# GELU by one ScalarE function in place of square, cubic, tanh and product steps, in a two-layer trunk

## The chip, the cores and the metric

The program runs on one core of a Trainium2 chip. The metric is the device time of one launch in microseconds; all data is fp32. The engines are named as in the profile: PE is TensorE (PEld its weight loads), DVE VectorE, ACT ScalarE, POOL GpSimd, SP the engine that issues the large DMAs.

## The reference

Two trunk layers run over 128 context and 512 latent tokens of width 1024. Each has a mixing sub-layer, which the change does not touch, and this expert sub-layer, in which every token picks 128 of 16384 single-neuron experts (8 heads of 16):

```python
def peer_ffn(h, p):
    ...
        g = jax.nn.softmax(best, axis=-1).astype(x.dtype)
        act = jax.nn.gelu(jnp.einsum('nhkd,nd->nhk', U[idx], x))
        return jnp.einsum('nhk,nhkd->nd', g * act, V[idx])
```

`jax.nn.gelu` is by default the tanh form, 0.5 a (1 + tanh(0.79788 (a + 0.044715 a^3))).

## The kernel before

The 640 tokens are five tiles of 128. Each layer's expert stage (`stage_experts`) computes them in two ways at once.

**Fetched tiles** (0, 1, 2). GpSimd gathers the rows of `peer_u` and then of `peer_v` for slot k of all 128 tokens, 512 KB a gather, into a ring of buffers (13, later 8). VectorE takes a dot product of each u row (`dot`, L2283) into one column of `acts`. When the 128 columns are there, `cube` makes a(1 + 0.044715 a^2) in three small VectorE steps for each half of 64 columns, ScalarE takes the tanh (L1928), and `weigh` forms (tanh + 1) times (0.5 a share) in two more. Then the v rows are summed with these weights: for tile 0 by TensorE, with diagonal matrices that ScalarE makes (L2006, L2221), for tiles 1 and 2 by VectorE (`add_row`, L2315). A ring buffer is free for the next gather when its row has been used.

**Dense, streamed tiles** (3, 4). All 16384 experts are computed for the 256 tokens, in 128 blocks of 128 experts. SP streams a block's part of both tables, 512 KB each; four u parts and three v parts are buffered. For block b:

- TensorE: `dense_products(b)` (L2202, 16 instructions) into one of two PSUM banks, when `keep_block(b - 2)` has freed it.
- ScalarE, `keep_block(b)`: the tanh of block b - 1 (L1979), then a copy of the products (L1992) and their scaled square (L1993) from PSUM.
- VectorE, `dense_block(b)`: first `gate_acts(b - 1)` (L2348), which multiplies (tanh + 1) into block b - 1 and so releases it to TensorE; then L2356, (square + 1) times a; then L2361, a times the gates (the factor 0.5 is in the gates).
- TensorE: `dense_sums(b)` (L2212, 8 instructions) adds the block's 128 x 1024 product to four PSUM banks.

TensorE's order is fixed: products(b), sums(b - 1), products(b + 1), sums(b). On VectorE and ScalarE the block work stands at fixed places among the rows: `BLOCK_BEHIND` puts block b behind row 40 + 3.66 b of the 512 rows of tiles 1 and 2 (u rows of tile 1 are 0 to 127, its v rows 128 to 255, tile 2 from 256 on). Rows 136 to 219 also carry the ranking of tile 2, one step a row, on VectorE (`rank_step`: maxima, indices and one-hot products, lines 1514 to 1612). Five softmaxes in a layer need ScalarE's Exp (`exp_best`, L1923), two of them amid the dense blocks.

Of the kernel before, what the change touches and what calls it, by code (L numbers as in the profile page):

```python
# [15 lines left out]
ALU = mybir.AluOpType  # L16
# [3 lines left out]
P = 128  # L20
# [1648 lines left out]
def stage_experts(nc, m, l):  # L1669
# [14 lines left out]
    with stage(nc) as sem:  # L1684
# [18 lines left out]
        cube_ready, tanh_ready, gelu_steps, weights_ready = sem("cube_ready"), sem("tanh_ready"), sem("gelu_steps"), sem("weights_ready")  # L1703
# [5 lines left out]
        acts_kept, inner_ready, acts_gated, act_tanh, acts_ready, v_used = (sem(f"dense_{n}") for n in (  # L1709
            "acts_kept", "inner_ready", "acts_gated", "tanh_ready", "acts_ready", "block_added"))  # L1710
# [16 lines left out]
        with nc.Block() as block:  # L1727
            @block.sync
            def _(eng):
# [29 lines left out]
                def load_gates(g):  # L1759
                    if g >= 2:  # L1760
                        eng.wait_ge(acts_gated, GROUP * (g - 1))
# [93 lines left out]
            def _(eng):  # L1855
# [69 lines left out]
                def tanh(i, h):  # L1925
                    cubed = m.cube[:, h * HALF:(h + 1) * HALF]
                    eng.wait_ge(cube_ready, 2 * i + h + 1)
                    eng.activation(cubed, cubed, ACT.Tanh, scale=0.7978845608028654).then_inc(tanh_ready, 1)  # L1928

                def keep_turned(d):  # L1930
# [4 lines left out]
                    eng.activation(m.slot_rows[:, 2, at], m.ps[:, 6 + u % 2, 2 * P:3 * P], ACT.Copy, scale=0.5)  # L1935
                    eng.activation(m.minus_share[:, at], m.ps[:, 6 + u % 2, 2 * P:3 * P], ACT.Copy, scale=-0.5).then_inc(
# [40 lines left out]
                def dense_tanh(b):  # L1977
                    eng.wait_ge(inner_ready, b + 1)
                    eng.activation(m.dense_inner[b % 2], m.dense_inner[b % 2], ACT.Tanh, scale=0.7978845608028654).then_inc(act_tanh, 1)  # L1979

                def keep_block(b):
                    u = block_unit(b)
                    acts = m.ps[:, 6 + u % 2, 0:NT]
                    if b > 0:
                        dense_tanh(b - 1)
                    else:
                        for stored in gates_stored:
                            eng.wait_ge(stored, 16 * CHUNKS // 2)
# [3 lines left out]
                    eng.activation(m.dense_acts[b % 2], acts, ACT.Copy).then_inc(acts_kept, 1)  # L1992
                    eng.activation(m.dense_inner[b % 2], acts.rearrange("p (d t) -> p d t", d=ND), ACT.Square, scale=0.044715 ** 0.5).then_inc(  # L1993
# [3 lines left out]
                tanh(0, 0)  # L1997
                eng.wait_ge(weights_ready, 1)
                for k in range(SLOTS):
                    if k == DIAGS:  # L2000
                        tanh(0, 1)
# [671 lines left out]
```

## Time and profile before

| | |
|---|---|
| time, median of 3 runs | 4896.74 us (4895.52 to 4900.41) |
| the profiled execution | 4902.44 us, of which 4900.6 us is its span |
| PE, PEld busy | 4319.5 us (88%), 2775.0 us (57%) |
| DVE busy | 3534.7 us (72%), 7391 instructions |
| ACT busy | 1158.6 us (24%), 2886 instructions |
| POOL busy | 2105.7 us (43%) |
| DMA | 1280.08 MB, mean 261 GB/s |
| granted TensorE clock, mean | 0.935 |

In a timeline or wait row, the bracket behind an instruction says how long its engine sat idle before it and what ended that idle time. In rows by stretch the DMA share is that of 16 DMA engines; values slightly over 1 are full. The dense blocks take 1480 to 2469 us of the span in the first layer and 3887 to 4875 us in the second.

### The profile page before, as it was taken

How to read it: one execution, taken by the hardware profiler on the slowest of the kernel's cores; microseconds unless marked ns; L12 is line 12 of the kernel's file. 1: busy time of each engine (PE TensorE's matmuls, PEld its weight loads, DVE VectorE, ACT ScalarE, POOL GpSimd, SP SyncE). 2: the span in 40 equal slices, each digit the busy share in tenths (PEclk: the TensorE clock that was granted, in tenths of full speed). 3: DMA queues.
4: the chain of work that ended last, by engine and by line, in shares of the span. 5: the costliest groups of instructions: out<-in, count | busy, mean ns of one | idle time of the engine just before them, and what ended most of it. 6: DMA issues, size and time to landing. Idle time of an engine off the chain costs nothing. (4 is left out here: it accounts for less than half of the span.)

```text
span 4900.6 us, 51932 instructions
## 1 busy us (share of the span) xinstructions
PE 4319.5 (88%) x17506; PEld 2775.0 (57%) x17506; DVE 3534.7 (72%) x7391; ACT 1158.6 (24%) x2886; POOL 2105.7 (43%) x1842
## 2 busy tenths in 40 slices
PE   8989969999848989999979898899996598899998
PEld 3368847544445555655544786565454465555655
DVE  6947665896587898777730676669956788977777
ACT  2112252214551111111110223422254411111111
POOL 0013240764345556665510233326643365566654
PEclk9999969999959999999989998799997799999999
DMA  8700011997689999999931000049976899999998
GB/s 304 240 18 2 1 54 61 337 400 275 241 289 365 408 363 390 407 408 403 405 142 40 6 1 20 35 148 385 368 271 242 303 397 392 365 404 401 407 407 342
DMA packets 390559, 1280.08 MB, mean 261 GB/s; under 512 B 39693, under 2 KB 79749, under 8 KB 387479
## 3 DMA queue, kind: packets, MB, share of 16 engines
q0 software_dynamic: 221184, 805.40, 43.3%
q1 hardware_dynamic: 169112, 471.36, 25.5%
q8 instruction: 142, 2.33, 0.2%
q14 instruction: 121, 0.98, 0.1%
HBM read 1235.01 MB, written 38.99 MB: 260 GB/s over the span
## 5 line engine op out<-in xcount | busy, mean ns | idle before, releaser
L1851 POOL DMA_INDIRECT z<-in_peer_v,experts x768 | 885.3, 1153 | 732.1 <-DVE w L2315 371.8
L1851 POOL DMA_INDIRECT z<-in_peer_u,experts x768 | 883.6, 1151 | 729.4 <-DVE state L2283 451.9
L2202 PE MATMUL ps<-hT,z 128*128 128x256 f32 x4096 | 930.1, 380 | 49.4 <-DMA z<-in_peer_ut 48.9
L2202 PEld LDWEIGHTS ps<-hT,z 128*128 128x128 f32 x4096 | 780.9, 191 | 264.3 <-issue 169.5
L2212 PE MATMUL ps<-w 128*128 128x512 f32 x1360 | 644.7, 618 | 113.2 <-DVE w L2348 112.8
L2315 DVE SCALAR_TENSOR_TENSOR w<-z,state,w 128x1024 f32<-128x1024 f32 x508 | 651.0, 1281 | 76.3 <-DMA z<-in_peer_v,experts 54.7
L2283 DVE CUSTOM_DVE_ANT_0 z<-z,o 128x1024 f32<-128x1024 f32 x512 | 611.6, 1219 | 82.6 <-DMA z<-in_peer_u,experts 81.0
L2212 PEld LDWEIGHTS ps<-w 128*128 128x128 f32 x1360 | 257.2, 196 | 414.6 <-issue 258.2
L2221 PE MATMUL ps<-z,o 128*128 128x512 f32 x1024 | 454.8, 597 | 17.5 <-ACT o L2006 17.5
L1992 ACT ACTIVATE w<-ps 128x256 f32<-128x256 f32 x256 | 98.1, 383 | 1511.5 <-PE ps L2202 1511.5
L2212 PE MATMUL ps<-z,w 128*128 128x512 f32 x688 | 327.7, 621 | 66.0 <-DVE w L2348 64.4
L2221 PEld LDWEIGHTS ps<-z,o 128*128 128x128 f32 x1024 | 190.9, 192 | 232.6 <-issue 232.6
L2283 DVE CUSTOM_DVE_ANT_0 z<-z,ps 128x1024 f32<-128x1024 f32 x256 | 306.0, 1213 | 22.5 <-DMA z<-in_peer_u,experts 19.1
L2356 DVE SCALAR_TENSOR_TENSOR hT<-hT,w 128x256 f32<-128x256 f32 x256 | 109.5, 428 | 278.2 <-ACT hT L1993 278.0
L2187 PE MATMUL ps<-w,z 128*128 128x128 f32 x1024 | 186.9, 346 | 117.7 <-DVE z L2340 70.9
L2187 PEld LDWEIGHTS ps<-w,z 128*128 128x128 f32 x1024 | 173.9, 252 | 161.4 <-issue 147.7
L2212 PEld LDWEIGHTS ps<-z,w 128*128 128x128 f32 x688 | 130.2, 196 | 221.3 <-issue 133.8
L848 POOL TENSOR_TENSOR kn<-kn,neg_half 128x4 f32<-128x4 f32 x20 | 20.1, 1007 | 486.2 <-DVE kn L891 457.6
L464 DVE SCALAR_TENSOR_TENSOR o<-gate,cond,o 128x1024 f32<-128x1024 f32 x160 | 192.4, 1276 | 12.5 <-DMA gate<-in_w_mod 12.5
L401 PE MATMUL ps<-w,hT 128*128 128x512 f32 (+1 forms) x480 | 189.8, 553 | 4.1 <-ACT hT L323 4.1
L583 PE MATMUL ps<-w,hT 128*128 128x512 f32 (+1 forms) x480 | 182.8, 543 | 0.9 <-DVE hT L555 0.9
L858 POOL TENSOR_TENSOR w<-w,const 128x512 f32<-128x512 f32 x60 | 86.5, 1448 | 209.7 <-DVE w L880 117.7
(450 smaller groups left out, 6288.3 us busy)
## 6 DMA issues: line engine op xcount, KB each, us to landing
z<-in_peer_ut SPq DMA_DIRECT2D x256, 512.0 KB, 8.4
w<-in_peer_v SPq DMA_DIRECT2D x170, 512.0 KB, 7.4
z<-in_peer_v SPq DMA_DIRECT2D x86, 512.0 KB, 7.3
gate<-in_w_mod SPq DMA_DIRECT2D x80, 512.0 KB, 4.8
w<-in_w_in SPq DMA_DIRECT2D x10, 2048.0 KB, 10.3
dense_gates<-w SPq DMA_DIRECT2D x8, 2048.0 KB, 9.7
dense_gates<-z SPq DMA_DIRECT2D x8, 2048.0 KB, 10.0
w<-dense_gates SPq DMA_DIRECT2D x16, 1024.0 KB, 18.5
```

Source lines behind the costliest of these rows:

```text
L401: mm = eng.matmul(m.ps[:, 4 + i % 4, 0:cols], m.hT[:, c, t * P:(t + 1) * P], m.w[n % 2][:, c, 0:cols], start=(c == 0), stop=(c == KC - 1))
L464: eng.scalar_tensor_tensor(total, m.mod_piece[i % BUFFERS], m.cond[:, c, s:s + 1], m.mod_bias if c == 0 else total, ALU.mult, ALU.add).the ...
L583: mm = eng.matmul(m.ps[:, 4 + i % 4, 0:cols], m.hT[:, c, k * P:(k + 1) * P], m.w[n % 2][:, c, 0:cols], start=(c == 0), stop=(c == KC - 1))
L1851: eng.indirect_dma_start(slot, None, at_layer_rows(table), bass.IndirectOffsetOnAxis(ap=m.experts[:, i % 2, k:k + 1], axis=0)).then_inc(lo ...
L1992: eng.activation(m.dense_acts[b % 2], acts, ACT.Copy).then_inc(acts_kept, 1)
L2187: mm = eng.matmul(to[:, i * P:(i + 1) * P], m.second_onehot[n % 2][:, i, :], m.first_onehot[n % 2][:, i, :], start=True, stop=True)
L2202: mm = eng.matmul(to[:, 0:NT], m.table_u[b % TABLE_U][:, c, :], m.hT[:, c, D0:TOK], start=(c == 0), stop=(c == KC - 1))
L2212: mm = eng.matmul(m.ps[:, 2 * d + n, :], m.dense_acts[b % 2][:, d * P:(d + 1) * P], m.table_v[b % TABLE_V][:, n * 512:(n + 1) * 512], star ...
L2221: mm = eng.matmul(m.ps[:, 4 + n, :], m.diag[:, k % DIAGS, :], row_j[:, n * 512:(n + 1) * 512], start=(k == 0), stop=(k == SLOTS - 1))
L2283: eng.tensor_tensor_reduce(row_j, row_j, h_first_rows if i == 0 else m.h_row, 1.0, 0.0, ALU.mult, ALU.add, m.acts[:, k:k + 1]).then_inc(us ...
L2315: ins = eng.scalar_tensor_tensor(m.row_sum, row_j, m.weight[:, k:k + 1], m.row_sum, ALU.mult, ALU.add)
L2356: eng.scalar_tensor_tensor(inner, inner, 1.0, acts.rearrange("p (d t) -> p d t", d=ND), ALU.add, ALU.mult).then_inc(inner_ready, 1)
```

## The change

For fetched tiles, `cube` and its three VectorE steps per half go; ScalarE's `gelu(i, h)` reads the dots and writes their GELU to the buffer `cube`, waiting only for the dots; `weigh` is one product with the share. For dense blocks, `keep_block` is one ScalarE instruction that reads PSUM and writes the GELU to `dense_acts`; `dense_block` is the one product with the gates, which now itself releases the block to TensorE; `gate_acts`, `dense_tanh`, the buffer `dense_inner` and four semaphores go. The factor 0.5 leaves the gates' scale.

```diff
-                def tanh(i, h):
-                    cubed = m.cube[:, h * HALF:(h + 1) * HALF]
-                    eng.wait_ge(cube_ready, 2 * i + h + 1)
-                    eng.activation(cubed, cubed, ACT.Tanh, scale=0.7978845608028654).then_inc(tanh_ready, 1)
+                def gelu(i, h):
+                    at = slice(h * HALF, (h + 1) * HALF)
+                    eng.wait_ge(used_v, rows_used(2 * i * SLOTS + (h + 1) * HALF - 1)[0])
+                    eng.activation(m.cube[:, at], m.acts[:, at], ACT.Gelu_apprx_tanh).then_inc(gelu_ready, 1)
...
-                def dense_tanh(b):
-                    eng.wait_ge(inner_ready, b + 1)
-                    eng.activation(m.dense_inner[b % 2], m.dense_inner[b % 2], ACT.Tanh, scale=0.7978845608028654).then_inc(act_tanh, 1)
-
                 def keep_block(b):
...
                     eng.wait_ge(*unit_made("unit", u))
                     if b >= 2:
                         eng.wait_ge(v_used, b - 1)
-                    eng.activation(m.dense_acts[b % 2], acts, ACT.Copy).then_inc(acts_kept, 1)
-                    eng.activation(m.dense_inner[b % 2], acts.rearrange("p (d t) -> p d t", d=ND), ACT.Square, scale=0.044715 ** 0.5).then_inc(
+                    eng.activation(m.dense_acts[b % 2], m.ps[:, 6 + u % 2, 0:NT], ACT.Gelu_apprx_tanh).then_inc(
                         unit_kept.sem, unit_kept.one("unit", u))
...
                 def weigh(i, h):
-                    acts = half(m.acts, h)
-                    eng.wait_ge(cube_ready, 2 * i + h + 1)
-                    o.after(0)
-                    gelu(eng.scalar_tensor_tensor(acts, acts, 0.5, half(m.share, h), ALU.mult, ALU.mult))
                     if i > 0:
                         eng.wait_ge(used_t, SLOTS)
-                    eng.wait_ge(tanh_ready, 2 * i + h + 1)
-                    eng.scalar_tensor_tensor(half(m.weight, h), half(m.cube, h), 1.0, acts, ALU.add, ALU.mult).then_inc(weights_ready, 1)
+                    o.after(0)
+                    eng.wait_ge(gelu_ready, 2 * i + h + 1)
+                    eng.tensor_tensor(half(m.weight, h), half(m.cube, h), half(m.share, h), ALU.mult).then_inc(weights_ready, 1)
...
                 def dense_block(b):
-                    if b > 0:
-                        gate_acts(b - 1)
-                    acts, inner = m.dense_acts[b % 2], m.dense_inner[b % 2]
-                    eng.wait_ge(acts_kept, b + 1)
                     eng.wait_ge(*unit_kept("unit", block_unit(b)))
-                    eng.scalar_tensor_tensor(inner, inner, 1.0, acts.rearrange("p (d t) -> p d t", d=ND), ALU.add, ALU.mult).then_inc(inner_ready, 1)
-                    eng.wait_ge(inner_ready, b + 1)
...
-                    eng.tensor_tensor(acts, acts, gate_part(b), ALU.mult).then_inc(acts_gated, 1)
+                    acts = m.dense_acts[b % 2].rearrange("p (c t) -> p c t", c=CHUNKS)
+                    eng.tensor_tensor(acts, acts, gate_part(b), ALU.mult).then_inc(acts_ready, 1)
```

What stands in a row on the engines, at three places. First VectorE, among the v rows of tile 1 that also carry ranking steps. Before (L2315 is one row, L2348 to L2361 a block's work):

```order
L2348 SCALAR_TENSOR_TENSOR w<-hT,w 128x256
L2356 SCALAR_TENSOR_TENSOR hT<-hT,w 128x2x128
L2361 TENSOR_TENSOR w<-w 128x256
L2315 SCALAR_TENSOR_TENSOR w<-z,state,w 128x1024
L1594 TENSOR_SCALAR ints<-ints 128x2x16
L2315 SCALAR_TENSOR_TENSOR w<-z,state,w 128x1024
```

After (L2327 is the product with the gates, L2294 one row):

```order
L2327 TENSOR_TENSOR w<-w 128x256
L2294 SCALAR_TENSOR_TENSOR w<-z,state,w 128x1024
L1594 TENSOR_SCALAR ints<-ints 128x2x16
L2294 SCALAR_TENSOR_TENSOR w<-z,state,w 128x1024
L1596 TENSOR_SCALAR ints<-ints 128x2x16
```

Of a block's three VectorE instructions one is left. Next ScalarE, around the last Exp of the layer (L1923), amid the dense blocks. Before:

```order
L1992 ACTIVATE w<-ps 128x256
L1993 ACTIVATE hT<-ps 128x2x128
L1923 ACTIVATE o<-o 128x128
L1979 ACTIVATE hT<-hT 128x2x128
L1992 ACTIVATE w<-ps 128x256
```

After (L1984 is the GELU of a block, L1922 the Exp):

```order
L1984 ACTIVATE w<-ps 128x256 x5
L1922 ACT_TABLE_LOAD
L1922 ACTIVATE o<-o 128x128
L1984 ACT_TABLE_LOAD
L1984 ACTIVATE w<-ps 128x256 x29
```

Three instructions a block became one, and the Exp now stands between two table loads that were not there. The whole program has 16 such loads in place of one: each layer has seven (before the first GELU of tile 0, before the Exp of the second softmax, before the GELU of block 0, and on both sides of two Exps amid the blocks), and the second layer begins its Exps with one. Last, the end of the second layer on VectorE. Before:

```order
L2356 SCALAR_TENSOR_TENSOR hT<-hT,w 128x2x128
L2361 TENSOR_TENSOR w<-w,rows 128x256
L2315 SCALAR_TENSOR_TENSOR w<-z,state,w 128x1024 x7
L2348 SCALAR_TENSOR_TENSOR w<-hT,w 128x256
L2320 TENSOR_TENSOR o<-w,gate 128x1024
```

After:

```order
L2294 SCALAR_TENSOR_TENSOR w<-z,state,w 128x1024 x4
L2327 TENSOR_TENSOR w<-w,rows 128x256
L2294 SCALAR_TENSOR_TENSOR w<-z,state,w 128x1024 x7
L2299 TENSOR_TENSOR o<-w,gate 128x1024
L2300 TENSOR_TENSOR x<-x,o 128x1024
```

The release of the last block to TensorE (L2348) stood behind the last seven rows; now it is L2327, ahead of them.

## Rows read from the trace of the kernel before

**Rows 1.** The page's first part: busy us, share of the span, instructions by engine.

```profile
PE 4319.5 (88%) x17506; PEld 2775.0 (57%) x17506; DVE 3534.7 (72%) x7391; ACT 1158.6 (24%) x2886; POOL 2105.7 (43%) x1842
```

**Rows 2.** Dense-block stretches: length, busy by engine, clock, DMA share, GB/s.

```profile
1679.70:1866.50 186.80, 159.90 (x537) 100.71 (x536) 174.40 (x383) 24.61 (x68) 98.19 (x80) 0.98 0.99 373
...
3887.40:4086.60 199.20, 182.48 (x613) 116.06 (x612) 162.61 (x353) 28.84 (x82) 118.96 (x95) 0.98 1.00 387
4086.60:4273.00 186.40, 159.47 (x535) 100.57 (x534) 173.98 (x382) 24.20 (x67) 97.36 (x79) 0.98 0.99 374
4273.00:4874.60 601.60, 563.21 (x1898) 358.94 (x1897) 451.71 (x671) 85.42 (x241) 361.30 (x289) 0.99 1.02 403
...
4300.00:4340.00 40.00, 38.35 (x135) 25.14 (x135) 31.41 (x37) 6.03 (x17) 26.50 (x21) 1.00 1.03 411
```

**Rows 3.** The same, VectorE's line 2361 (one per dense block) alone.

```profile
4086.60:4273.00 186.40, 8.94 (x22) 0.98 0.99 374
4273.00:4874.60 601.60, 34.02 (x80) 0.99 1.02 403
```

**Rows 4.** VectorE's waits (us, times, longest): two stretches, then whole span.

```profile
DVE hT L2356 <- ACT hT L1993: 11.5, 8, 2.2
...
DVE hT L2356 <- ACT hT L1993: 86.5, 65, 4.5
...
DVE o L2320 <- PE ps L2212: 8.5, 2, 4.5
```

**Rows 5.** Timeline of one dense block: start, length, instruction, idle before.

```profile
4177.90 0.41 DVE L2348 SCALAR_TENSOR_TENSOR w<-hT,w 128x256 f32<-128x256 f32 x1
4178.24 0.42 DVE L2356 SCALAR_TENSOR_TENSOR hT<-hT,w 128x256 f32<-128x256 f32 x1
...
4178.37 3.70 PE L2212 MATMUL ps<-z,w 128*128 128x512 f32 x8 [1.35 <-DVE w L2348]
...
4178.69 0.42 DVE L2361 TENSOR_TENSOR w<-w 128x256 f32<-128x256 f32 x1
...
4179.03 1.28 DVE L2315 SCALAR_TENSOR_TENSOR w<-z,state,w 128x1024 f32<-128x1024 f32 x1
...
4181.91 3.62 PE L2202 MATMUL ps<-hT,z 128*128 128x256 f32 x16
...
4185.56 0.38 ACT L1992 ACTIVATE w<-ps 128x256 f32<-128x256 f32 x1 [6.46 <-PE ps L2202]
...
4186.33 0.43 DVE L2356 SCALAR_TENSOR_TENSOR hT<-hT,w 128x256 f32<-128x256 f32 x1 [0.43 <-ACT hT L1993]
```

**Rows 6.** Timeline of the second layer's end.

```profile
4874.58 0.42 DVE L2361 TENSOR_TENSOR w<-w,rows 128x256 f32<-128x256 f32 x1
...
4874.93 9.62 DVE L2315 SCALAR_TENSOR_TENSOR w<-z,state,w 128x1024 f32<-128x1024 f32 x7
...
4884.46 0.42 DVE L2348 SCALAR_TENSOR_TENSOR w<-hT,w 128x256 f32<-128x256 f32 x1
...
4884.93 6.71 PE L2212 MATMUL ps<-w 128*128 128x512 f32 x8 [7.35 <-DVE w L2348]
```

**Rows 7.** Timeline of the start of tile 0's weighted sum, second layer.

```profile
3480.47 0.31 ACT L1923 ACTIVATE o<-o 128x128 f32<-128x128 f32 x1 [4.37 <-DVE o L1550]
...
3482.40 0.26 ACT L1928 ACTIVATE state<-state 128x64 f32<-128x64 f32 x1 [1.62 <-DVE state L2295]
...
3483.42 2.44 ACT L2006 ACTIVATE o<-const,state 128x128 f32<-128x128 f32 x8 [0.76 <-DVE state L2305]
...
3483.92 5.33 PE L2221 MATMUL ps<-z,o 128*128 128x512 f32 x7 [8.46 <-ACT o L2006]
```

**Rows 8.** Timeline of ScalarE at the span's start.

```profile
0.73 1.28 ACT L305 ACT_TABLE_LOAD   x1 [0.73 <-PEq L2667]
```

**Rows 9.** The chain that ended last, 4255 to 4300: start, length, what.

```profile
4256.05 3.70 PE ps L2212 x8
...
4272.66 5.40 PE ps L2212 x8
```

More of the change, by code:

```diff
@@ L1708, in stage_experts @@
         u_loaded, v_loaded = [sem(f"table_u_loaded{k}") for k in range(TABLE_U)], [sem(f"table_v_loaded{k}") for k in range(TABLE_V)]
-        acts_kept, inner_ready, acts_gated, act_tanh, acts_ready, v_used = (sem(f"dense_{n}") for n in (
-            "acts_kept", "inner_ready", "acts_gated", "tanh_ready", "acts_ready", "block_added"))
+        acts_ready, v_used = sem("dense_acts_ready"), sem("dense_block_added")
         def place_of(j):
@@ L1991, in keep_block @@
                         eng.wait_ge(v_used, b - 1)
-                    eng.activation(m.dense_acts[b % 2], acts, ACT.Copy).then_inc(acts_kept, 1)
-                    eng.activation(m.dense_inner[b % 2], acts.rearrange("p (d t) -> p d t", d=ND), ACT.Square, scale=0.044715 ** 0.5).then_inc(
+                    eng.activation(m.dense_acts[b % 2], m.ps[:, 6 + u % 2, 0:NT], ACT.Gelu_apprx_tanh).then_inc(
                         unit_kept.sem, unit_kept.one("unit", u))
                 exp_best(0)
-                tanh(0, 0)
+                gelu(0, 0)
                 eng.wait_ge(weights_ready, 1)
@@ L2000, in _ @@
                     if k == DIAGS:
-                        tanh(0, 1)
+                        gelu(0, 1)
                     if k == HALF:
@@ L2020, in _ @@
                     if k % (2 * SLOTS) == HALF + 2:
-                        tanh(1 + k // (2 * SLOTS), 0)
+                        gelu(1 + k // (2 * SLOTS), 0)
                     if k == SHARES_BEHIND[3]:
@@ L2031, in _ @@
                     if k % (2 * SLOTS) == SLOTS - 1:
-                        tanh(1 + k // (2 * SLOTS), 1)
-                dense_tanh(NKEY - 1)
+                        gelu(1 + k // (2 * SLOTS), 1)
             @block.tensor
@@ L2244, in _ @@
                 h_first_rows = m.ps[:, 0:2, :].rearrange("p b n -> p (b n)")
-                o, gelu, res = Order(eng, route_steps), Order(eng, gelu_steps), Order(eng, sums)
+                o, res = Order(eng, route_steps), Order(eng, sums)
                 def gate_output(i):
@@ L2417, in _ @@
                         dense_block(b)
-                cube(1, 1)
                 for k in range(SLOTS):
@@ L2595, in place @@
     m.dense_acts = [wall[:, 7168 + b * NT:7168 + (b + 1) * NT] for b in range(2)]
-    m.dense_inner = [m.hT[:, ND * b:ND * (b + 1), 0:P] for b in range(2)]
     m.table_u = [zall[:, (8 + b) * D:(9 + b) * D].rearrange("p (c n) -> p c n", c=KC) for b in range(TABLE_U)]
```

33 lines of the change are left out of this document (5 added, 28 removed).

## The prediction

> **What bounds the kernel now.** I read the busy shares first, then the dense-block stretches one by one, then VectorE's waits, then the timeline of one block. Over the whole span TensorE is busy 88%, VectorE 72%, ScalarE only 24% [rows 1], so shortening ScalarE's work alone gains nothing. The changed block code runs in some 990 us of each layer, and there the question is what sets the pace. Away from the ranking steps a 40 us window moves 411 GB/s at a DMA share of 1.03 [rows 2]: the transfers are full, and 411 is my measure of full. Over 601.6 us the last stretch still averages 403 [rows 2], and its blocks come every 601.6 / 79 = 7.6 us (80 records, the first and the last at its edges) [rows 3]. In such a stretch a faster VectorE cannot help. The middle stretch differs: 22 blocks in 186.4 us [rows 3], 8.5 us each, at 374 GB/s in the second layer and 373 in the first, with VectorE busy 174 of 186 us [rows 2]. These are the rows that also carry tile 2's ranking. VectorE is late there, a late row frees its ring buffer late, and the next gather starts late. The remaining 11.5 us of VectorE's time there are one wait, for ScalarE's square of the block's products [rows 4].
>
> The block's timeline shows why VectorE waits on anything. Its first instruction, L2348 at 4177.90, releases the previous block; TensorE, idle for 1.35 us by then, runs the sums (4178.37) and the next products (4181.91), ScalarE gets them at 4185.56, and VectorE's L2356, ready earlier, waits 0.43 us and starts at 4186.33 [rows 5]. So TensorE waits for VectorE once a block, and VectorE for TensorE and ScalarE once a block, in turn.
>
> **The change, part by part.**
>
> *VectorE in a dense block.* L2348 starts at 4177.90, and the row behind the block's three instructions at 4179.03: 1.13 us. L2361 alone takes 4178.69 to 4179.03, 0.34 us [rows 5]. So 0.79 us a block goes, 17.4 us over the middle's 22 blocks.
>
> *The lockstep.* sums(b) is now released by block b's own product, one place of 3.66 rows earlier. TensorE can run the next products while VectorE does rows, and VectorE should find its GELU made. This takes away most of the 11.5 us in the middle, and of the 86.5 us in the last stretch [rows 4]; what is late next there is the rows, by the full DMA.
>
> *Middle stretch.* VectorE's own bound falls to 186.4 - 11.5 - 17.4 = 157.5 us, 7.2 us a block. The transfers' bound is 186.4 x 374 / 411 = 169.6 us, so it decides: at most 16.8 us saved, and in the first layer 186.8 x (1 - 373 / 411) = 17.3 us. The low end is 0, if the gathers' round trip and not VectorE sets the pace. I take 13 a layer, nearer the high end, since VectorE's 94% busy leaves little room for another cause: 26 us.
>
> *First and last stretch.* By the same reckoning 199.2 x (1 - 387 / 411) = 11.6 us and 601.6 x (1 - 403 / 411) = 11.7 us are missing from full [rows 2]. The first has more VectorE work than the last (the ranking of tile 1 among its rows), so I take a third of the one, 4 us, and a sixth of the other, 2 us, and as much in the first layer: 12 us together. Their ends are 0 and 47.
>
> *The end of a layer.* Now L2348 stands behind the last seven rows: it starts at 4884.46, TensorE has been idle 7.35 us and takes 6.71 us for the last eight instructions instead of 3.70 [rows 5, 6], and VectorE waits 8.5 us in all, in two places, 4.5 us at most, for these sums before it can add them [rows 4]. After the change the release stands ahead of the seven rows, which take 9.62 us [rows 6]; the sums fit under them. Both waits go whole: 8.5 us. What is late next is VectorE's own residual steps.
>
> *ScalarE.* A block's three instructions become one of about 0.38 us [rows 5]. On the path only the second PSUM read counts, about 0.3 us, and it lies under the transfers: nothing.
>
> *Fetched tiles.* The five small VectorE steps of a half become one. At the start of tile 0's sum, from the end of the Exp (3480.78) to ScalarE's first diagonal (3483.42) there are 2.6 us [rows 7] with the steps of both halves. Of that TensorE waits for all, so it is worth costing: after the Exp a table load of 1.28 us [rows 8] and a GELU of 0.26 us end at 3482.3, and one product and the diagonal follow, about 0.8 us earlier than now. The other five halves of a layer stand among rows and cost under 1.3 us each (half of those 2.6); they lie under the transfers. Nothing for all; bounds 15 us of gain, 3 of loss.
>
> *Table loads.* The order of ScalarE shows 15 new ones. The one load in the trace takes 1.28 us [rows 8]. All but the one just costed stand where ScalarE idles: between blocks it is idle 6.46 us [rows 5], and during the diagonals eight are made ahead. So 0 to 15 x 1.28 = 19 us of loss; I take 0.
>
> The Trainium skill, "ScalarE: Activation LUTs", section "What ACT_TABLE_LOAD costs", gives 1283 ns for the load and about 1380 ns more for a drain, 2.66 us a switch, and its section "Table sets: the hidden batching unit" says to batch calls by set, which this change does the opposite of. The row agrees on the load; no row here shows the drain. By the page the upper end of the loss is an estimated 40 us, which would leave 6 of the 46 us below, and the first diagonal would come 0.6 us later rather than 0.8 earlier.
>
> *New waits.* `gelu(i, h)` waits on ScalarE for the dots of its half with block GELUs queued behind it, and TensorE behind those. They wait only if TensorE is ahead of VectorE's rows by then, that is for something that is not late: nothing. SP's table loads stay in their order.
>
> **Sum.** 26 + 12 + 8.5 = 46.5 us, from the profiled execution's 4902.4: 4856. That execution is 5.7 us above the median of the runs shown (4896.7), so **4850 us**.
>
> **Rivals.**
>
> *The transfers hide it all.* If the pace of the middle is the gathers' round trip, VectorE's 28.9 us become idle time and only the ends of the layers gain, 8.5 us: 4888. For it: GpSimd's gathers are 8 deep at most. Against it: the same ring gives 411 GB/s elsewhere [rows 2].
>
> *The table loads are exposed.* 19 us of the 46.5 are given back: 4869. Against it: ScalarE's idle gaps.
>
> *The transfers fill up everywhere.* All that is missing from full is recovered, 34 + 47, and 8.5 at the ends: 4896.7 - 89 = 4807. Against it: the last stretch is held up by its own mix of transfers too, which nothing here changes.
>
> *TensorE loses its clock; slower.* TensorE now runs ahead and then stands idle in every block. The clock is granted at 0.98 in all stretches [rows 2], but single sums at the lower level (1.2 in place of 2.4 GHz, in part) take 5.40 us in place of 3.70 [rows 9]. From start to start a block costs TensorE 3.54 + 3.65 = 7.2 us [rows 5]. The pace now is 987.2 us for 127 blocks, 7.8 us. If more than one block in three pays the 1.7 us, TensorE is slower than that; with every second, 8.05 us a block, 254 blocks lose 71 us less the 8.5: about 4959. Against it: in the middle stretch TensorE is already idle 27 of 186 us, at 0.98 [rows 2].
>
> **How the numbers follow.** The forecast's case, 4828 to 4866, has 0.72; the exposed loads (whose time lies in the range) 0.07; the full transfers, where they pass 4828, 0.06; all hidden 0.10; slower 0.05. Under 4828 and over 4882 lie 0.19, so the range is 4828 to 4882. A measurement of this kernel tells 0.2%, about 10 us, from no change. Faster by more: 0.72 + 0.07 + 0.06 = 0.85; within it 0.10; slower 0.05.
>
> **What would show it.** Right: the middle stretch at 170 to 175 us and over 400 GB/s; VectorE's wait for ScalarE there and in the last stretch nearly gone, with waits for fetched rows in its place; no idle time before the last residual steps; 16 table loads, next to none of them waited for. Wrong: a middle stretch of the old length with an idle VectorE (then the gathers' round trip sets it), a granted clock under 0.95 in the stretches, or loads of which VectorE or TensorE waits for more than a few.

## The result, and the profile after

| | before | after |
|---|---|---|
| median of 4 runs | 4896.13 us (4892.95 to 4900.41) | 4830.85 us (4829.40 to 4835.61) |
| ratio, 95% interval | | 0.9868 (0.9851 to 0.9885) |
| profiled execution | 4902.44 us | 4831.36 us |

The change saves 65 us by the medians, 71 us between the two profiled executions. The forecast was 4850 us; the measured time is 19 us below it and inside its range. Mechanism and sign were right, two terms of the sum were too small, and one step was wrong in a way that the time of the changed kernel alone doesn't show.

The page's busy shares of the changed kernel, which answer to [rows 1], and three of its groups (busy us, mean ns of one, idle time ahead of them and what ended it):

```profile
PE 4298.0 (89%) x17506; PEld 2774.6 (57%) x17506; DVE 3339.4 (69%) x6831; ACT 1002.6 (21%) x2389; POOL 2022.9 (42%) x1842
...
L2294 DVE SCALAR_TENSOR_TENSOR w<-z,state,w 128x1024 f32<-128x1024 f32 x508 | 651.2, 1282 | 251.4 <-DMA z<-in_peer_v,experts 245.0
L2273 DVE CUSTOM_DVE_ANT_0 z<-z,o 128x1024 f32<-128x1024 f32 x512 | 623.8, 1222 | 285.3 <-DMA z<-in_peer_u,experts 282.6
...
L1984 ACT ACTIVATE w<-ps 128x256 f32<-128x256 f32 x256 | 98.3, 384 | 1728.2 <-PE ps L2192 1728.2
```

VectorE lost 195 us of work, and over the whole span it now waits some 530 us in its rows for fetched data. The same three stretches of the second layer as in [rows 2], cut where the product with the gates (now L2327) of blocks 0, 26, 48 and 127 begins; columns as in [rows 2]:

```profile
3848.90:4040.10 191.20, 182.25 (x625) 118.53 (x624) 143.04 (x292) 13.27 (x31) 109.41 (x94) 0.99 1.02 403
4040.10:4211.40 171.30, 158.66 (x544) 102.05 (x543) 158.16 (x339) 10.83 (x25) 106.49 (x80) 0.99 1.03 407
4211.40:4808.00 596.60, 561.25 (x1880) 359.39 (x1880) 392.37 (x506) 32.45 (x83) 317.56 (x290) 0.98 1.03 406
```

Before, these moved 387, 374 and 403 GB/s; now all three move 403 to 407, and the first layer's 400, 406 and 406. The granted clock moved by no more than 0.01. VectorE's longest waits in the middle and in the last of these stretches (engine, what it waited for, us in all, times, longest), against [rows 4]:

```profile
DVE w L2294 <- DMA z<-in_peer_v,experts: 13.4, 20, 1.2
...
DVE w L2294 <- DMA z<-in_peer_v,experts: 106.0, 124, 2.2
DVE z L2273 <- DMA z<-in_peer_u,experts: 93.4, 99, 1.5
```

No wait for ScalarE is left in either; 11.5 and 86.5 us of it stood there. VectorE now waits for rows. TensorE still waits for VectorE's product with the gates, 12.2 us in the middle and 30.6 us in the last stretch, where it waited 26.7 and 39.7 us for L2348 before. The chain of work that ended last shows what stands behind VectorE: in the last stretch 81% of it is gathers of rows in flight; before, these were 30% of it, and TensorE's instructions 39%.

**Where the 71 us went.** The stretches between the same products, in us:

| from block to block | before, layers 1 and 2 | after | saved |
|---|---|---|---|
| 0 to 26 (first) | 199.7, 198.7 | 191.8, 191.2 | 7.9, 7.5 |
| 26 to 48 (middle) | 186.8, 186.9 | 168.5, 171.4 | 18.3, 15.5 |
| 48 to 127 (last) | 602.4, 601.6 | 596.8, 596.5 | 5.6, 5.1 |
| last product to the residual steps of layer 1, to the span's end in layer 2 | 16.75, 26.0 | 12.5, 21.3 | 4.25, 4.7 |

That is 59.9 us in the dense stretches and 9.0 at the layers' ends. Block 0 of the first layer comes 4.8 us earlier, of which 3.5 are there ahead of the first instruction that the change touches, so they are no part of it; 2.4 us are lost between layer 1's residual steps and block 0 of layer 2. 59.9 + 9.0 + 4.8 - 2.4 = 71.3. Without the 3.5 the profiled pair gives 67.8, near the 65 of the medians. The rest of the 4.8 is not shown to come from the change either: in a second profile of the kernel before, *before_again* below, block 0 comes at 1473.2 us, ahead of the changed kernel's 1475.3.

### The profile page after: what moved, and what is told of

It is laid out like the page before. It is cut to its first block and busy times, and to the rows that moved or that the text cites. A ratio compares the mean times of both kernels' runs of the same rounds, so it can differ in the third digit from the quotient of the medians.

```text
span 4829.3 us, 50351 instructions
## 1 busy us (share of the span) xinstructions
PE 4298.0 (89%) x17506; PEld 2774.6 (57%) x17506; DVE 3339.4 (69%) x6831; ACT 1002.6 (21%) x2389; POOL 2022.9 (42%) x1842
## 5 line engine op out<-in xcount | busy, mean ns | idle before, releaser
L1850 POOL DMA_INDIRECT z<-in_peer_v,experts x768 | 851.6, 1109 | 733.2 <-DVE w L2294 371.0
L1850 POOL DMA_INDIRECT z<-in_peer_u,experts x768 | 834.2, 1086 | 750.7 <-DVE state L2273 501.2
L2294 DVE SCALAR_TENSOR_TENSOR w<-z,state,w 128x1024 f32<-128x1024 f32 x508 | 651.2, 1282 | 251.4 <-DMA z<-in_peer_v,experts 245.0
L2273 DVE CUSTOM_DVE_ANT_0 z<-z,o 128x1024 f32<-128x1024 f32 x512 | 623.8, 1222 | 285.3 <-DMA z<-in_peer_u,experts 282.6
L1984 ACT ACTIVATE w<-ps 128x256 f32<-128x256 f32 x256 | 98.3, 384 | 1728.2 <-PE ps L2192 1728.2
L858 POOL TENSOR_TENSOR hT<-hT,const 128x512 f32<-128x512 f32 x60 | 85.6, 1433 | 199.4 <-DVE hT L880 103.7
## 6 DMA issues: line engine op xcount, KB each, us to landing
z<-in_peer_ut SPq DMA_DIRECT2D x256, 512.0 KB, 10.6
```

The lines of the kernel that those rows point to most:

```text
L858: eng.tensor_tensor(heads4(m.ct[d][j % 2][:, :]), m.lh[d][:, :].rearrange("p (h k x) -> p h k x", h=4, k=2)[:, :, 0, :], bc(const(m, f"lev ...
L1850: eng.indirect_dma_start(slot, None, at_layer_rows(table), bass.IndirectOffsetOnAxis(ap=m.experts[:, i % 2, k:k + 1], axis=0)).then_inc(lo ...
L1984: eng.activation(m.dense_acts[b % 2], m.ps[:, 6 + u % 2, 0:NT], ACT.Gelu_apprx_tanh).then_inc(unit_kept.sem, unit_kept.one("unit", u))
L2273: eng.tensor_tensor_reduce(row_j, row_j, h_first_rows if i == 0 else m.h_row, 1.0, 0.0, ALU.mult, ALU.add, m.acts[:, k:k + 1]).then_inc(us ...
L2294: ins = eng.scalar_tensor_tensor(m.row_sum, row_j, m.weight[:, k:k + 1], m.row_sum, ALU.mult, ALU.add)
```

## The experiments

**Theory.** In the kernel before, the dense stretches were held under the transfers' ceiling by a lockstep of TensorE, ScalarE and VectorE. The change takes three things out of it: VectorE's 0.79 us a block, the late release, and ScalarE's second read of PSUM. With enough of them gone the transfers set the pace at some 407 GB/s, and more gives nothing. **Rivals:** one of the three alone carries the gain; the table loads cost part of what could be had; the fetched tiles' shorter chain carries a part; the ceiling is not the transfers but something else that the change left alone.

Each kernel was timed beside the kernel before on the same chip, and a ratio is to that. The chips differ: the kernel before takes 5009 and 5011 us where late_release, vector_steps_back, both_back, dense_only, no_switch and loads_moved ran, and 4895 to 4898 us elsewhere. In the changed kernels that were profiled on both kinds of chip, the difference lies outside the dense stretches (block 0 of the first layer comes at 1519 to 1533 in place of 1475 us), so ratios and stretch lengths are compared below, and times across chips are not.

### One cause put back at a time

*late_release* is the changed kernel with the old place of the release: block b - 1 is released by a one-column copy at the start of block b's VectorE work.

```diff
+                def release(b):
+                    eng.wait_ge(acts_gated, b + 1)
+                    eng.tensor_copy(m.hT[:, 0, 0:1], m.dense_acts[b % 2][:, 0:1]).then_inc(acts_ready, 1)
                 def dense_block(b):
+                    if b > 0:
+                        release(b - 1)
...
-                    eng.tensor_tensor(acts, acts, gate_part(b), ALU.mult).then_inc(acts_ready, 1)
+                    eng.tensor_tensor(acts, acts, gate_part(b), ALU.mult).then_inc(acts_gated, 1)
```

> The changed kernel, but the release of a dense block to TensorE is again issued by VectorE one block later, by a copy of one column ahead of the next block's product (under 0.1 us of VectorE a block). VectorE's 0.79 us a block stays saved. Theory V (VectorE's freed time makes the gain): the middle stretch stays near 170 us and only the end of a layer loses its 4.5 us and a little elsewhere, 4840 to 4848 us. Theory R (the earlier release makes it): VectorE waits for the GELU of the block again as before, the first and last stretches fall back to 199 and 602 us and most of the gain goes, 4870 to 4890 us.

Measured: 0.9909 (0.9886 to 0.9933), 44.6 us less than before. Its middle stretch (columns as in [rows 2]):

```profile
4158.90:4331.80 172.90, 157.61 (x535) 100.00 (x533) 159.28 (x360) 10.40 (x25) 105.47 (x80) 0.99 1.02 400
```

And VectorE's only wait in it:

```profile
DVE w L2334 <- ACT w L1985: 15.1, 10, 2.6
```

The wait for ScalarE is back, 15.1 us, and the stretch still takes 172.9 us, 14.0 less than before: VectorE's own time went by 14.7 us, and that is what shows. The last stretches take 597.0 and 596.8 us, as in the changed kernel, though VectorE's wait for ScalarE is back there too (78.3 us in the second layer). The first stretches, 195.8 and 195.3 us, lie halfway between the changed kernel's 191.5 and the 199 of before. The second layer's end is back at 25.0 us after the last product, where the changed kernel has 21.3. So neither theory's time came: 0.9909 of 4896 us is 4851, between the 4840 to 4848 of V and the 4870 to 4890 of R.

*vector_steps_back* leaves the release early and puts two VectorE steps of a block's size back, behind the product and on another buffer, so that VectorE has its old work and nothing waits for it but the rows.

```diff
                     eng.tensor_tensor(acts, acts, gate_part(b), ALU.mult).then_inc(acts_ready, 1)
+                    for k in range(2):
+                        eng.wait_ge(padded, 2 * b + k)
+                        eng.scalar_tensor_tensor(m.hT[:, 2:4, 0:P], m.hT[:, 0:2, 0:P], 1.0, m.hT[:, 0:2, 0:P], ALU.add, ALU.mult).then_inc(padded, 1)
```

> The changed kernel with the early release, but two VectorE steps of 128x256 that nobody needs behind each dense block's product (some 0.8 us a block, as before the change). Theory V: the middle stretch goes back towards 186 us in each layer, 4850 to 4865 us, while first and last stretch keep their gain, since VectorE now waits there for fetched rows. Theory R: no change, 4829 to 4838 us.

Measured: 0.9874 (0.9853 to 0.9895), 58.8 us less. Its middle stretch, in which VectorE's only wait is one of 1.3 us for a fetched row:

```profile
4159.60:4334.30 174.70, 157.25 (x536) 99.69 (x536) 173.80 (x384) 10.41 (x24) 98.59 (x80) 1.00 1.02 398
```

VectorE works 173.8 of 174.7 us: there it is the bound, at what the kernel before leaves without its 11.5 us of waiting, 186.9 - 11.5 = 175.4. So with ScalarE's shorter turn beside it, either of VectorE's two causes gives most of the middle (14.0 and 12.3 us in the second layer, against 15.5 for all of it), and they don't add up, because the transfers stand close behind either. No run has one of them without ScalarE's part.

On the whole time theory R's forecast came: 0.9874 of 4896 us is 4834, and the interval overlaps the changed kernel's, so the time doesn't show that VectorE's saved steps are worth anything beside the early release. Only the stretches do: in sum they take 1923.5 us, where the changed kernel's take 1916.1. The middle ones are longer by 6.6 and 3.2 us and the first by 1.6 and 2.2, but the last ones are shorter, 592.7 and 594.3 in place of 596.8 and 596.5 us, at a granted clock of 0.99 and 1.00 in place of 0.98. No run explains that.

*both_back* has both: the release late, by a step of the old size, and one step ahead of the product. What is left of the change in a block is ScalarE's side: one instruction in place of three, one read of PSUM in place of two.

```diff
+                    eng.scalar_tensor_tensor(acts, acts, 1.0, acts, ALU.mult, ALU.max).then_inc(acts_ready, 1)
...
                 def dense_block(b):
+                    if b > 0:
+                        release(b - 1)
...
+                    eng.scalar_tensor_tensor(m.hT[:, 2:4, 0:P], m.hT[:, 0:2, 0:P], 1.0, m.hT[:, 0:2, 0:P], ALU.add, ALU.mult).then_inc(padded, 1)
+                    eng.wait_ge(padded, b + 1)
```

> The changed kernel with both taken back: one padding step ahead of the product, and the release one block late by a full-size step. What is left of the change is ScalarE's single function and the fetched tiles. If the two parts explain the gain: 4885 to 4896 us, with the stretches at their old lengths. If ScalarE's shorter work counts for itself: 4860 to 4880 us.

Measured: 0.9959 (0.9945 to 0.9973), 20.8 us less than before. The stretches are 196.6 and 195.8, 185.6 and 184.5, 598.7 and 598.6 us: most of the way back to the kernel before, not all. The middle one moves 380 GB/s. In the last stretch VectorE waits for ScalarE again, less than the 86.5 us before (another 10.4 us ahead of the same instruction have no releaser in the profile):

```profile
DVE hT L2334 <- ACT w L1985: 61.3, 50, 3.9
```

So 0.4% is left that neither of VectorE's two causes holds, as the second forecast, 4860 to 4880 us, had it. The prediction had given nothing to what remains.

*scalar_too* is both_back with the second read: a Square of the products behind the GELU, into a buffer that nothing uses, and only this frees the PSUM bank and starts VectorE.

```diff
-                    eng.activation(m.dense_acts[b % 2], m.ps[:, 6 + u % 2, 0:NT], ACT.Gelu_apprx_tanh).then_inc(
+                    eng.activation(m.dense_acts[b % 2], m.ps[:, 6 + u % 2, 0:NT], ACT.Gelu_apprx_tanh)
+                    eng.activation(m.hT[:, 4 + 2 * (b % 2):6 + 2 * (b % 2), 0:P], m.ps[:, 6 + u % 2, 0:NT].rearrange("p (d t) -> p d t", d=ND), ACT.Square).then_inc(
                         unit_kept.sem, unit_kept.one("unit", u))
```

> The kernel of both_back with one thing more taken back: ScalarE reads each dense block's products from PSUM a second time (a square that nobody uses, 0.28 us more until the block is released to VectorE and the bank to TensorE). both_back kept 0.4% of the 1.4% gain, 16 us of it in the dense stretches. If that rest is ScalarE's shorter turn: the time comes back to that of before, ratio 0.998 to 1.000. If the rest is something else (the tanh step, the fetched tiles): ratio 0.995 to 0.997 as in both_back.

Measured: 0.9996 (0.9987 to 1.0005), over 11 and 15 runs: 4894.05 against 4895.32 us. The time of the kernel before is back; the stretches take 1970.7 us in sum, and 1976.1 and 1973.2 in the two profiles of the kernel before. The timeline of scalar_too around the end of one block's products:

```profile
4185.06 0.42 DVE L2327 SCALAR_TENSOR_TENSOR w<-w 128x256 f32<-128x256 f32 x1
...
4185.15 0.38 ACT L1985 ACTIVATE w<-ps 128x256 f32<-128x256 f32 x1 [7.86 <-PE ps L2194]
4185.43 0.38 ACT L1986 ACTIVATE hT<-ps 128x256 f32<-128x256 f32 x1
...
4185.53 3.70 PE L2204 MATMUL ps<-w 128*128 128x512 f32 x8 [0.42 <-DVE w L2327]
4185.84 0.43 DVE L2335 SCALAR_TENSOR_TENSOR hT<-hT 128x256 f32<-128x256 f32 x1 [0.36 <-ACT hT L1986]
```

And VectorE's longest wait in its last stretch, against 86.5 us before:

```profile
DVE hT L2335 <- ACT hT L1986: 77.7, 61, 2.9
```

VectorE starts when the second read ends, 4185.81, and not when the first does: 4185.43 - 4185.15 = 0.28 us later in each block. 0.28 x 256 blocks would be 72 us if all of it counted. By the ratios of both_back and scalar_too it counts for some 0.4%, about 18 us, and their intervals don't overlap. Of these 18, the six stretches show 10.8 (1959.9 and 1970.7 us in sum); where the others lie was not found. What the second read alone would cost in the changed kernel, where the transfers are full, no run shows.

### The fetched tiles

*dense_only* has the change in the dense blocks alone. The fetched tiles keep `cube`, the tanh and the two steps of `weigh`:

```diff
-                    eng.wait_ge(used_v, rows_used(2 * i * SLOTS + (h + 1) * HALF - 1)[0])
-                    eng.activation(m.cube[:, at], m.acts[:, at], ACT.Gelu_apprx_tanh).then_inc(gelu_ready, 1)
+                    eng.wait_ge(cube_ready, 2 * i + h + 1)
+                    eng.activation(cubed, cubed, ACT.Tanh, scale=0.7978845608028654).then_inc(tanh_ready, 1)
```

> The change made for the dense blocks alone; the fetched tiles keep square, cubic, tanh and product steps (tanh without a table load more, if it is in the same table as the new function). If the fetched tiles are worth nothing, as predicted: 4829 to 4836 us, at most 2 us for the two starts of tile 0's sum. If their small steps on VectorE count: 4840 us or more.

Measured: 0.9848 (0.9824 to 0.9872). The full change gave 0.9868 and, run again, 0.9864. The interval takes both in, and its stretches (192.2 and 190.1, 170.7 and 171.4, 594.3 and 598.3 us) are the full change's within 3 us each and 1 us in sum. The fetched tiles' part is worth nothing that can be measured, as forecast; the interval would hide some 12 us.

### The table loads

*no_switch* takes the loads away: the five softmaxes of a layer use Tanh in place of Exp, so that their shares are not the reference's, and from tile 0's first GELU on ScalarE needs no other set of functions in the expert stage. 4 loads are left of 16, two of them ahead of that first GELU.

```diff
-                    eng.activation(m.shifted, m.shifted, ACT.Exp).then_inc(sems.best_exp_ready, 1)
+                    eng.activation(m.shifted, m.shifted, ACT.Tanh).then_inc(sems.best_exp_ready, 1)
```

> The changed kernel with the softmax's exponential in the expert stage replaced by tanh (so its shares are not the reference's): only 4 table loads are left of 16. If the 12 loads are exposed: 12 x 1.28 = 15 us less, 4815 us. If they are hidden but for the one ahead of block 0 of each layer, where ScalarE loads only after it has waited for the products: 2 to 3 us less, 4828 us.

Measured: 0.9865 (0.9843 to 0.9887), the changed kernel's ratio. Twelve loads fewer, nothing gained: 15 us less would have given about 0.984. A gain of 2 to 3 us is too small for this interval.

*loads_moved* keeps them and moves them off the waits: a one-column GELU ahead of block 0's wait, and the two Exps amid the blocks issued behind the next block's GELU.

```diff
                     if b == 0:
+                        eng.activation(m.hT[:, 0, 0:1], const(m, "ident", 0, 1), ACT.Gelu_apprx_tanh)
...
-                    if k == SHARES_BEHIND[3]:
-                        exp_best(3)
```

> The changed kernel with a GELU of one column ahead of the wait for block 0's products, so that its table load runs during that wait, and with the two Exps amid the dense blocks issued behind the next block's GELU instead of ahead of it, so that the GELU no longer stands behind ScalarE's wait for the ranking (9.0 and 9.8 us in the second layer). If the transfers set the pace everywhere: 2 to 3 us less (the load ahead of block 0), 4828 us. If the block held behind the Exp costs a stall of its own: 3 to 8 us less, 4823 to 4828 us.

Measured: 0.9858 (0.9836 to 0.9881). Between the two kernels lie 2 us of 4942; both say that the loads cost nothing measurable. In loads_moved block 0's load does stand ahead of ScalarE's wait for the products, and the Exps wait at most 2.0 us in place of 6.1 to 10.6. In the trace of the changed kernel ScalarE looks like this ahead of block 0 of the second layer, and around the Exp at the middle stretch's end:

```profile
3847.16 1.28 ACT L1984 ACT_TABLE_LOAD   x1 [28.44 <-PE ps L2192]
3848.46 0.38 ACT L1984 ACTIVATE w<-ps 128x256 f32<-128x256 f32 x1
...
4202.98 1.28 ACT L1922 ACT_TABLE_LOAD   x1
4213.30 0.31 ACT L1922 ACTIVATE o<-o 128x128 f32<-128x128 f32 x1 [9.04 <-DVE o L1550]
4213.62 1.28 ACT L1984 ACT_TABLE_LOAD   x1
4214.92 0.38 ACT L1984 ACTIVATE w<-ps 128x256 f32<-128x256 f32 x1
```

The first of these loads comes behind ScalarE's wait of 28.44 us, not in it, and so delays block 0 by its 1.28 us. The second is made while ScalarE waits for VectorE's shares, and is covered. The third stands between the Exp and a GELU whose products were ready since 4211.2 (TensorE's products run from 4207.62 for 3.62 us), which comes 3.7 us late by the wait and the load. So the first and the third kind have no idle gap of ScalarE's over them.

### Is it the transfers that set the pace now?

*half_v* and *half_v_before* stream half of each `peer_v` block (256 of 512 KB) in the changed kernel and in the one before; the other half of the sums is made from what lies in the buffer, so the output is not the reference's. The work of all engines stays.

```diff
-                    eng.dma_start(m.table_v[b % TABLE_V], m.inp["peer_v"][l, b * P:(b + 1) * P, :]).then_inc(v_loaded[b % TABLE_V], 16)
+                    eng.dma_start(m.table_v[b % TABLE_V][:, 0:512], m.inp["peer_v"][l, b * P:(b + 1) * P, 0:512]).then_inc(v_loaded[b % TABLE_V], 16)
```

> The changed kernel with only the first 512 of 1024 columns of each dense block's part of peer_v loaded (so the second half of the dense tiles' sums is made with stale data); 256 KB of some 3 MB less to move in each block, all engines' instructions as before. If the transfers set the pace now: the last stretch falls by up to 8%, from 597 us to TensorE's own pace of 7.2 us a block, 568 us. If something else sets it: 597 us.

> The kernel before with the same half load (same stale half). If its last stretch was held by the transfers alone, it falls to 568 us too. If the turn-taking of TensorE, ScalarE and VectorE held a share of it, which I now think, it falls less, to 580 to 592 us; and the middle stretch, held by VectorE, stays at 185 to 187 us.

Measured, one run each: 4683.5 and 4812.3 us. Middle and last stretch of the second layer, of half_v and then of half_v_before:

```profile
3952.00:4110.60 158.60, 157.50 (x553) 103.92 (x552) 157.20 (x340) 10.80 (x25) 108.96 (x80) 1.00 1.03 404
4110.60:4660.00 549.40, 543.08 (x1882) 356.40 (x1881) 392.50 (x506) 32.28 (x83) 354.42 (x290) 1.00 1.03 403
```

```profile
4030.50:4218.40 187.90, 160.55 (x535) 101.22 (x534) 174.35 (x382) 24.62 (x68) 97.75 (x80) 0.97 0.94 338
4218.40:4785.10 566.70, 554.05 (x1898) 358.08 (x1898) 448.88 (x672) 85.45 (x241) 389.83 (x290) 0.99 1.01 392
```

VectorE's longest wait in the last stretch of half_v_before:

```profile
DVE hT L2356 <- ACT hT L1993: 101.0, 77, 4.0
```

With lighter transfers the changed kernel's middle stretch falls from 170.7 (after_again, below) to 158.6 us, and VectorE is busy 157.2 of them: it has come to its own bound, which the prediction had worked out as 157.5. The last stretch falls from 597.6 to 549.4 us. The number of gathers is the same and the rate stays at 403 and 404 GB/s, so the time follows the bytes: by rate times length 7.8% fewer in the middle and 8.7% fewer in the last stretch, which got 7.1% and 8.1% shorter. A pace set by the round trip of single gathers would not have changed. The middle stretch of the kernel before doesn't get shorter at all (186.9, now 187.9), though it moves only 338 GB/s, 17% under the full rate: VectorE's work and its waits in the lockstep held it, not the transfers. Between the two kernels now lie 129 us in place of 66 (one run each). So the transfers cap what the change gives, and with half of one table gone it would be worth twice as much. The last stretches were both shorter than expected. In half_v TensorE is busy 543 of 549 us, and a block takes 6.95 us, where 7.2 had been worked out from [rows 5]; TensorE's own bound and the transfers' lie together there.

The forecast for half_v_before missed: the turn-taking was to leave 580 to 592 us, and 566.7 came, which is near the 568 named for transfers alone. Both figures had been worked out with 7.2 us a block, so they don't decide it. The pair does: with the lighter transfers the kernel before still takes 17 us more than the changed one (566.7 against 549.4), moves 392 GB/s, and VectorE waits 101 us for ScalarE. But the lockstep alone needs no more than 567 us for this stretch, and the transfers need 597 in the changed kernel. So in the kernel before the last stretch, 600 to 602 us, was set by the transfers in the main, and by the lockstep only in the last 5 us. In the middle stretch it was the other way round.

### Both kernels again, and a better version

*before_again* and *after_again* are the two kernels unchanged, on the chip of half_v.

> The kernel before, profiled on the same chip as the three others of this group, to have its stretches beside theirs. Both theories: first, middle and last stretch near 199, 187 and 602 us, as in the first profile, whatever the rest of the program takes on this chip.

> The changed kernel unaltered, on the same chip. Its time over that of before: 0.986 to 0.988 as first measured; stretches near 192, 170 and 597 us.

Measured: after_again 0.9864 (0.9848 to 0.9881), stretches 191.8 and 190.6, 168.5 and 170.7, 596.8 and 597.6 us; before_again 4892.5 us, 199.2 and 199.0, 186.9 and 186.9, 601.2 and 600.0. The stretches repeat within 2 us. The second layer's end takes 24.9 us in before_again, where it took 26.0 in the first profile, because TensorE's last eight instructions take 5.69 in place of 6.71 us, at a granted clock of 0.65 in place of 0.55.

*later_end* is loads_moved with the dense blocks spread over four more rows of the 512, so that fewer rows stand behind the last block:

```diff
-FIRST_ROW, LAST_ROW, LATE_TURN = 40, 508, 200
+FIRST_ROW, LAST_ROW, LATE_TURN = 40, 512, 200
```

> The kernel of loads_moved, with the 128 dense blocks spread to row 512 instead of row 508, so that three rows and not seven stand behind the last block. If the last rows were held by VectorE while the transfers had run out, the end of a layer gains 1 to 4 us; if the last block's sums come into the open again, it loses as much. Within 4 us of loads_moved either way.

Measured: 0.9851 (0.9835 to 0.9868), 4825.27 us (4824.94 to 4827.95) against 4898.03. Its end:

```profile
4807.60 0.42 DVE L2327 TENSOR_TENSOR w<-w,rows 128x256 f32<-128x256 f32 x1
4807.94 4.06 DVE L2294 SCALAR_TENSOR_TENSOR w<-z,state,w 128x1024 f32<-128x1024 f32 x3
...
4808.08 3.70 PE L2202 MATMUL ps<-w 128*128 128x512 f32 x8 [2.54 <-DVE w L2327]
...
4812.03 1.22 DVE L2299 TENSOR_TENSOR o<-w,gate 128x1024 f32<-128x1024 f32 x1
```

From the last product to the end it takes 15.8 us in place of 21.3, for three rows behind the last block in place of seven; the stretches take 1926.7 us in all in place of 1916.1, part of it the four rows a layer that moved ahead of the last block. All four of its runs (4824.94 to 4827.95 us) lie below all eight of the changed kernel (4829.08 to 4835.61), but on another chip, and the intervals of the ratios overlap (dense_only's ratio is as low, 0.9848), so the step from one to the other is not shown.

## Why the prediction was right, and where it was wrong

**Middle stretch: the mechanism right, the term too small.** 26 us forecast, 33.8 measured. The wait for ScalarE went, waits for rows came, and the rate rose to 406 and 407 GB/s, as forecast. VectorE's bound was right too (157.5 worked out; 158.2 busy here, 157.2 in half_v). What was mis-sized is the fraction: 13 of 17 us were taken, out of caution about VectorE being busy 94% (by the rows 93%), while nothing held back any of it. In the first layer even more came, 18.3 us, than the 17.3 that the formula allows; the stretch moved 68.4 MB in place of 69.7, so bytes shifted between neighbouring stretches, and the bound holds for their sum rather than for each. One reading was too strong: "once a block" the two engines were to wait for each other, but in the middle stretch TensorE waits for VectorE 16 times and VectorE for ScalarE 8 times in 22 blocks.

**First and last stretch: too small.** 12 us forecast, 26.1 measured. A third and a sixth of what is missing from full had been taken, with no row to choose them by. 15.4 us came in the first stretches and 10.7 in the last, of 23.2 and 23.4 that were missing by that measure. The other error ran against this one: 411 GB/s was the peak of a 40 us window, and the most that full transfers hold as an average over a whole stretch is 407 here. That is known only from the changed kernel. With 407 the prediction's own formula gives 199.2 x (1 - 387 / 407) = 9.8, 186.4 x (1 - 374 / 407) = 15.1 and 601.6 x (1 - 403 / 407) = 5.9 us, 61.6 in both layers; 59.9 were measured. By this ceiling nine tenths of what the last stretches missed came, and four fifths in the first, which move 400 and 403 GB/s and so are not quite full. So in the main the rival "the transfers fill up everywhere", which had a chance of 0.06, is what happened, at a lower ceiling than it was priced with: with the 8.5 of the ends it gives 4902.4 - 70.1 = 4832 for the profiled execution, which took 4831.4.

**The ends: right.** 8.5 us forecast, 9.0 measured, and late_release gives back 3.7 of the second layer's 4.7 (25.0 for 21.3), which is all of it by before_again's 24.9. Part of the gain is TensorE's clock, which the forecast took from the row without naming it: in the kernel before the last eight sums come behind 7.35 us of idle time and take 6.71 us at a granted clock of 0.55; in the changed kernel they come behind 1.37 us and take 3.70 us at 1.00. The sums lie under the seven rows, and VectorE's residual steps start without a wait:

```profile
4807.98 0.42 DVE L2327 TENSOR_TENSOR w<-w,rows 128x256 f32<-128x256 f32 x1
4808.31 9.61 DVE L2294 SCALAR_TENSOR_TENSOR w<-z,state,w 128x1024 f32<-128x1024 f32 x7
...
4808.45 3.70 PE L2202 MATMUL ps<-w 128*128 128x512 f32 x8 [1.37 <-DVE w L2327]
...
4817.95 1.23 DVE L2299 TENSOR_TENSOR o<-w,gate 128x1024 f32<-128x1024 f32 x1
...
4820.47 1.22 DVE L2299 TENSOR_TENSOR o<-ps,gate 128x1024 f32<-128x1024 f32 x1
```

**ScalarE: wrong.** The step read: on the path only the second PSUM read counts, about 0.3 us, and it lies under the transfers, nothing. Where the transfers are full it does; but in the lockstep of the kernel before they were not, and there the read stood between TensorE and VectorE in every block. both_back and scalar_too put it at about 18 us. In the sum it left no error that a run shows, because all of the change together runs into the transfers, whose bound had been worked out apart; that was luck as far as this step goes. As a statement on what ScalarE's part is worth, it was wrong.

**Table loads: the price right, the reason partly wrong.** 0 was taken for the fifteen, and no_switch shows 0, to within some 11 us. But the cover named, ScalarE's idle gaps, holds for some only; block 0's load in each layer is exposed by 1.28 us, and the GELU behind each Exp amid the blocks comes late by one. That they cost nothing all the same fits blocks that have slack while the transfers set the pace, but no run shows that cause apart. A load holds ScalarE for 1.28 us and no more: the next instruction starts 0.02 us after it in every place looked at.

```profile
1067.56 0.31 ACT L1922 ACTIVATE o<-o 128x128 f32<-128x128 f32 x1 [9.73 <-DVE o L1550]
1067.88 1.28 ACT L1927 ACT_TABLE_LOAD   x1
1069.18 0.26 ACT L1927 ACTIVATE state<-state 128x64 f32<-128x64 f32 x1
1069.79 2.44 ACT L1997 ACTIVATE o<-const,state 128x128 f32<-128x128 f32 x8 [0.36 <-DVE state L2284]
```

The Trainium skill, "ScalarE: Activation LUTs", section "What ACT_TABLE_LOAD costs", has a drain of about 1380 ns with every switch; the load's 1283 ns agree with the trace, the drain doesn't show, neither behind the load nor, at 0.01 us, ahead of it. The measurement decides: 1.28 us a switch.

**Fetched tiles: right.** From the Exp's end to the first diagonal it takes 1.9 us (1067.87 to 1069.79) in place of 2.6 [rows 7], 0.7 us less where 0.8 were forecast. dense_only shows no effect on the whole.

**New waits: one that was overlooked.** The forecast named `gelu(i, h)` as the wait that could hold block GELUs up. The one that does is the Exp amid the blocks: ScalarE stands 9.04 us at it (above), with the next block's GELU queued behind. It is not new, only longer: in the kernel before ScalarE stood 4.05 us at the same Exp. loads_moved takes these GELUs from behind it and gains nothing, so it costs nothing here.

**The rivals.** *The gathers' round trip* sets the pace: refuted, the middle stretch moves 407 GB/s, and in half_v it gets shorter with the same gathers. *TensorE loses its clock*: refuted, the granted clock is 0.97 to 0.99 in the six stretches, though TensorE still stands idle behind VectorE's rows. *Table loads exposed*, at 19 us: refuted by no_switch. Of the rivals on the change's parts, "one of the three causes carries it" is refuted for ScalarE's part, which without the other two gives 21 us (both_back). With it, VectorE's saved steps give 45 (late_release), and the early release gives 59 (vector_steps_back), which the time doesn't tell from the 65 of all three; with everything put back 1 is left. So the early release and the shorter turn carry nearly all, and the 195 us of VectorE's work that went are worth little beside them. Neither of VectorE's two parts was run quite alone.

**The chances.** The three rivals outside the range, 0.06, 0.10 and 0.05, add up to 0.21, where 0.19 was taken; the range and the forecast don't hang on it.

**What stays open.** The 7 of the 18 us of ScalarE's second read that the stretches don't show; why the first stretches stay at 400 and 403 GB/s; why vector_steps_back's last stretches are the shortest; the 2.4 us lost between the layers, of which block 0's load explains 1.28; and whether later_end beats the changed kernel.

## What to carry to other kernels

When several waits form one lockstep in front of a shared bound, price each part of a change by the bound that it runs into, and the whole change by that bound at once: parts that each look sufficient don't add up, and a part that "lies under the transfers" does so only once the transfers are full. Take the ceiling of a shared resource from a long full stretch, not from its best 40 us; and if the bound behind a stall has been worked out and no row speaks against reaching it, a fraction of it needs a reason (here the whole of it came). A change that meets such a ceiling is worth more beside one that lightens the resource (129 us in place of 66 here).

## What the runs showed of the hardware

- 400 to 407 GB/s over stretches of 170 to 600 us, in both layers, is what one core's transfers held in the changed kernel with gathers and streamed tables mixed; 411 was a 40 us peak.
- A table load takes 1.28 us, with 0.01 to 0.02 us on either side. Where the instruction that needs it follows a wait, the load is made after the wait, not in it (block 0), unless the wait stands between the load and its instruction (the Exps amid the blocks). In dense_only the fetched tiles' tanh runs in both neighbourhoods, beside Exp and beside the GELU, with 12 loads in all and none on its line.
- The same program differs by 110 us (2.3%) between chips: the kernel before takes 5009 and 5011 us on two of them, at a mean granted clock of 0.921 to 0.929, and 4895 to 4898 us on others, at 0.933 to 0.938. The dense stretches of no_switch and loads_moved, on the slower kind, are within 2 us of the changed kernel's elsewhere, so the difference lies outside them; what causes it no run shows.
